# Gather of four items at once from a two-part split of the unnormalised rows, extra items beside their expert, filler products on TensorE in the routing

## The reference

```python
for l in range(DEPTH):                                   # DEPTH = 1
    h = x + hybrid_mixer(rmsnorm(x, norm_mix_g[l]), ...)
    x = h + hierarchical_moe(rmsnorm(h, norm_ffn_g[l]), ...)
return rmsnorm(x, final_norm_g)

def hierarchical_moe(xn, rg_w, rg_b, re_w, re_b, w1, w3, w2):
    ...
    e_w = e_top / jnp.sum(e_top, axis=-1, keepdims=True) * g_top
    expert_id = g_idx * EXPERTS_PER_GROUP + e_idx        # 1 of 4 groups, 2 of its 8 experts
    gate = jnp.sum(jax.nn.one_hot(expert_id, N_EXPERTS, dtype=f32) * e_w[..., None], axis=1)
    h = jax.nn.silu(jnp.einsum('td,edf->tef', t, w1)) * jnp.einsum('td,edf->tef', t, w3)
    h = h * gate[:, :, None].astype(h.dtype)
    y = jnp.einsum('tef,efd->td', h, w2)
```

## Time and profile before

| what | value |
|---|---|
| median of 3 runs | 1475.35 us (1474.34 to 1475.4) |
| profiled execution, its own time | 1474.14 us |
| span from first to last instruction | 1472.3 us |
| mean granted TensorE clock | 0.985 |
| PE busy, share of the span | 94% |
| DVE, ACT, POOL busy | 37%, 25%, 15% |
| chain that ended last | PE 58%, DMA 21% |
| read from HBM | 481.53 MB |

### The profile page before, as it was taken

How to read it: one execution, slowest core, us unless ns; L and a number is a source line. 1 busy time by engine, 2 the same in 40 slices (tenths; PEclk the granted TensorE clock), 3 DMA queues, 4 the chain that set the end, 5 groups by cost and what they waited for, 6 DMA issues and landing times.

```text
span 1472.3 us, 20876 instructions
## 1 busy us (share of the span) xinstructions
PE 1379.7 (94%) x8358; PEld 786.9 (53%) x8358; DVE 540.8 (37%) x1072; ACT 366.5 (25%) x625; POOL 214.4 (15%) x198
## 2 busy tenths in 40 slices
PE   6999899998896899999999999999999999999996
PEld 5874697896685444443543444435434444354343
DVE  4899710415413523322323223223232232232325
ACT  3010168565555211111102111111021111110212
POOL 2000356576684100000000000000000000000000
PEclk9999999999998899999999999999999999999998
DMA  8433444334357599999999999999999999999993
GB/s 208 170 115 114 144 175 144 126 131 168 115 214 300 243 422 427 427 426 423 428 426 427 425 428 426 426 424 427 427 427 423 427 426 426 426 427 428 427 423 136
DMA packets 80682, 484.19 MB, mean 329 GB/s; under 512 B 17393, under 2 KB 17474, under 8 KB 46210
## 3 DMA queue, kind: packets, MB, share of 16 engines
q1 hardware_dynamic: 79842, 481.28, 80.1%
q10 hardware_dynamic: 672, 2.10, 0.4%
q0 software_dynamic: 128, 0.26, 0.1%
HBM read 481.53 MB, written 2.10 MB: 328 GB/s over the span
## 4 chain that ended last, share of the span: by engine, by line
PE 58%; DMA 21%; DVE 3%; ACT 2%; issue 1%; POOL 0%; DVEq 0%; ACTq 0%
PE ps L1750 22%; DMA ring<-in_expert_w_dram 21%; PE ps L1413 11%; PE ps L1768 9%; PE ps L1728 6%; PE ps L1758 3%; PE ps L1779 2%; PE ps L1780 1%; PE ps L1740 1%; ACT reg_t L786 1%; DVE reg_e L1074 0%; PE ps L1678 0%; DVE reg_y L1036 0%; ACT reg_d L785 0%; DVE reg_x L1356 0%
## 5 line engine op out<-in xcount | busy, mean ns | idle before, releaser
L1750 PE MATMUL ps<-ring,reg_y 128*64 128x512 f32 x1056 | 240.1, 598 | 31.6 <-DMA ring<-in_expert_w_dram 31.6
L1750 PE MATMUL ps<-reg_e,reg_y 128*64 128x512 f32 x1056 | 234.6, 593 | 0.8 <-DVE reg_y L1274 0.8
L1768 PE MATMUL ps<-ring,reg_y 128*64 128x512 f32 x1056 | 233.5, 595 | 0.8 <-DVE reg_y L1289 0.8
L528 POOL TENSOR_TENSOR w_lo<-ring,w_hi 128x512 fp32r<-128x512 f32 x144 | 183.6, 1303 | 90.8 <-ACT w_hi L585 89.1
L1295 DVE TENSOR_TENSOR y_lo_t<-ps,y_hi_t 64x512 fp32r<-64x512 f32 x132 | 90.9, 689 | 213.0 <-ACT y_hi_t L815 211.7
L1750 PEld LDWEIGHTS ps<-ring,reg_y 128*64 128x64 f32 x1056 | 70.6, 136 | 183.3 <-issue 128.8
L815 ACT ACTIVATE y_hi_t<-ps 64x512 fp32r<-64x512 f32 x132 | 78.1, 591 | 335.0 <-PE ps L1768 332.6
L1750 PEld LDWEIGHTS ps<-reg_e,reg_y 128*64 128x64 f32 x1056 | 74.6, 137 | 154.7 <-issue 143.4
L1768 PEld LDWEIGHTS ps<-ring,reg_y 128*64 128x64 f32 x1056 | 72.9, 137 | 134.7 <-issue 132.0
L1304 DVE TENSOR_TENSOR reg_x<-ps,reg_x 128x512 f32<-128x512 f32 x136 | 87.3, 684 | 121.6 <-PE ps L1780 121.6
L1285 DVE TENSOR_SCALAR reg_y<-ps,lamv 128x512 f32<-128x512 f32 x33 | 24.8, 751 | 256.4 <-PE ps L1750 256.4
(11 more groups left out here) (355 smaller groups left out, 1507.8 us busy)
## 6 DMA issues: line engine op xcount, KB each, us to landing
ring<-in_expert_w_dram SPq DMA_DIRECT2D x132, 2048.0 KB, 22.5
reg_e<-in_expert_w_dram SPq DMA_DIRECT2D x66, 2048.0 KB, 23.6
ring<-in_w_in_dram SPq DMA_DIRECT2D x20, 2048.0 KB, 8.0
ring<-in_w_out_dram SPq DMA_DIRECT2D x8, 2048.0 KB, 8.0
reg_x<-in_x_dram SPq DMA_DIRECT2D x4, 1024.0 KB, 8.4
out_dram<-reg_x SPq DMA_DIRECT2D x4, 512.0 KB, 2.7
reg_e<-in_ssm_w_glu_dram ACTq DMA_DIRECT2D x1, 1024.0 KB, 5.9
reg_d<-in_final_norm_g_dram ACTq DMA_DIRECT2D x1, 1024.0 KB, 4.7
```

The source lines that it names most:

```text
L528: G.tensor_tensor(w_lo[:, i % BUFS, :], unit(u % SLOTS_A)[:, c, :], w_hi[:, i % BUFS, :], ALU.subtract).then_inc(row_lo, 1)
L1750: last = M(psb[m][64 * i:64 * i + 64, :], xeT[:, cc, 64 * q:64 * q + 64], unit(s)[:, c, :], start=cc < 2, stop=cc >= DC - 2)
L1768: last = M(psb[3 + i // 2][64 * (i % 2):64 * (i % 2) + 64, :], hT[:, 2 * half + f, :], unit2(s)[:, f, 512 * i:512 * i + 512], start=half = ...
```

## The change

- Rows are split into two parts in the type that PE multiplies in one pass (`h_hi`, `h_lo`), straight from h without the factor 1/rms. ACT (`h_high`) and DVE (`h_low`) do it column group by column group as the last projections end. POOL has no part in it. The factor 1/rms is gathered with the gates and applied where ACT and DVE copy the results of w1 and w3 (`a_up`, `v_up`).
- `gather` serves four items (`QG`): 16 blocks x 2 parts x 2 halves = 64 products of 256 columns, once in two passes. `gates` sums two numbers a slot for four items. DVE makes `selS` from two numbers a token (`x_r`).
- Items stand in expert order: an extra item comes right after its expert's first item. SP loads an expert once (`item(first item's number, e)`); the slot of unit k is given back by the expert's last item. POOL watches the transfers and tells PE by `e_in`, which counts items, not experts. With 33 items, item 17 is the extra one of expert 16, and the one that is left for a pass of its own is item 32, expert 31.
- The router's chain loses the gates' placing and gains the items' numbering before the slots are chosen; numbers of extra items come later.
- `keep_clock` issues 6 and 3 products whose result nobody reads, before and behind the ranking.
- The rows of w2 are dealt to partitions in another order, so that each partition reads one run of memory a unit; ACT and DVE read the results of w1 and w3 with a step of four values for it.
- The last norm's weights are loaded by SP at the end, into a free weight slot.

```diff
+QG = 4
+HG = QG // QE
 ITERS = NE // QE
+GROUPS = NE // QG
 PASSES = T // SLOT
 EXTRA = 8
+ITEMS = NE + EXTRA
...
-        w2_v = e_w2.rearrange("l e (h c p) n -> p (l e) h c n", h=2, p=P)
+        w2_v = e_w2.rearrange("l e (p h c) n -> p (l e) h c n", h=2, p=P)
...
-            with sp.Fori(0, NE) as e:
-                item(e, e)
-            sp.wait_ge(rk_ready, 2)
...
+            item(0, 0)
+            sp.wait_ge(rk_ready, 1)
+            with sp.Fori(1, NE) as e:
+                item(sp.value_load(c_int[0:1, ds(e, 1)], min_val=1, max_val=ITEMS - 1), e)
+            sp.wait_ge(slot_free, (sp.value_load(n_extra[0:1, 0:1], min_val=0, max_val=EXTRA - 1) + NE) * 6 + 1)
+            sp.dma_start(fg, final_g.unsqueeze(0).broadcast_to([P, D])).then_inc(fg_in, 16)
...
+            def item_landed(e):
+
+                for k in range(6):
+                    s = slot_of(k)
+                    base = 16 * (UNITS_A // SLOTS_A) if s < SLOTS_A else 0
+                    g.wait_ge(ring_in[s], e * 16 + base + 16)
+                    g.sem_inc(e_in, 1)
+
+            item_landed(0)
+            g.wait_ge(rk_ready, 2)
+            with g.Fori(1, ITEMS) as i_:
+                item_landed(g.value_load(ids[0:1, ds(i_, 1)], min_val=0, max_val=NE - 1))
...
+            def h_high(k):
+                for b in range(TB):
+                    A.activation(h_hi[:, b, :, 32 * k:32 * k + 32], h_columns(b, k), cp).then_inc(hp_hi, 1)
...
-                A.activation(a1, psb[0][:, :], cp).then_inc(e_a1, 1)
+                a.wait_ge(e_gsev, g_ + 1)
+                A.activation(v3(a1, P), psb[0][:, :].rearrange("p (q f) -> p f q", f=EC), cp,
+                             scale=g_slot[:, q, 0:1]).then_inc(e_a1, 1)
...
+            def h_low(k):
+
+                v.wait_ge(hp_hi, TB * (k + 1))
+                for b in range(TB):
+                    V.tensor_tensor(h_lo[:, b, :, 32 * k:32 * k + 32], h_columns(b, k), h_hi[:, b, :, 32 * k:32 * k + 32],
+                                    ALU.subtract).then_inc(hp_lo, 1)
...
+            link(V.tensor_scalar(x_n, cnt, float(SLOT), 1.0, ALU.is_gt, ALU.add))
+            for k in range(2, PASSES):
+                link(V.scalar_tensor_tensor(x_n, cnt, float(SLOT * k), x_n, ALU.is_gt, ALU.add))
+            link(V.tensor_tensor_scan(x_e, ones[:, 0:NE], x_n, 0.0, ALU.mult, ALU.add))
+            link(V.scalar_tensor_tensor(x_p, x_c.unsqueeze(1).broadcast_to([P, TB, NE]), float(SLOT), rk, ALU.mult, ALU.add))
+            link(V.scalar_tensor_tensor(x_p, x_p, 1.0, sel, ALU.add, ALU.mult))
+            V.reduce_max(x_r[:, :, 0:1], x_p, axis=AX)
+            link(V.reduce_sum(x_sum, x_p, axis=AX))
+            link(V.tensor_tensor(x_r[:, :, 1:2], x_sum, x_r[:, :, 0:1], ALU.subtract))
...
+                w = nq * SLOT
+                out = [selS[:, b, 0:nq, :].rearrange("p q s -> p (q s)") for b in range(TB)]
                 for b in range(TB):
+                    last = V.tensor_scalar(out[b], iota_q[:, 0:w], x_r[:, b, 0:1], None, ALU.is_equal)
+                step(last, g_, 2)
...
+            def v_gather(g_, nq):
+                w = nq * SLOT
+                for m in range(DC // 2):
+                    v.wait_ge(e_gath, g_ * 8 + m + 1)
+                    V.tensor_tensor(xeT[m // 4][:, 2 * (m % 4):2 * (m % 4) + 2, 0:w],
+                                    v3(psb[(0, 1, 5)[m % 3]][:, :], QG * SLOT)[:, :, 0:w],
+                                    g_rows[:, 2 * m:2 * m + 2].unsqueeze(2).broadcast_to([P, 2, w]), ALU.mult).then_inc(e_gev, 1)
...
+            def keep_clock(n_):
+
+                for _i in range(n_):
+                    M(psb[7][:, :], ident[:, :], xt[:, 0, 0:512], start=True, stop=True)
+
+            keep_clock(6)
...
+            def gather(g_, nq):
+                w = nq * SLOT
+                pe.wait_ge(e_sel, g_ + 1)
...
-                    for part in (hi, mid, lo):
+                    for part in (h_hi, h_lo):
                         for b in range(TB):
-                            last = M(psb[bank][:, (c % 4) * P:(c % 4) * P + ns], part[:, b, c * P:(c + 1) * P],
-                                     selS[:, b, 0:ns // SLOT, :].rearrange("p q s -> p (q s)"), start=k == 0, stop=k == 5)
+                            last = M(bank[:, o:o + w], part[:, b, c, :], selS[:, b, 0:nq, :].rearrange("p q s -> p (q s)"),
+                                     start=k == 0, stop=k == 3)
...
+            keep_clock(3)
+            pe.wait_ge(hp_lo, 4 * TB)
+            pe.wait_ge(id_r, 1)
+            gather(0, QG)
+            pe_items(0, 0, 0, 0, QE, first=True)
+            for h in range(1, HG):
+                pe_items(h, 0, QE * h, h, QE)
+            with pe.Fori(1, GROUPS) as it:
+                for h in range(HG):
+                    pe_items(it * HG + h, it, it * QG + QE * h, h, QE)
```

More of the change, by code:

```diff
@@ L1749, in up @@
                         i = c % 2
-                        last = M(psb[m][64 * i:64 * i + 64, :], xeT[:, cc, 64 * q:64 * q + 64], unit(s)[:, c, :],
+                        last = M(psb[m][64 * i:64 * i + 64, :], xeT[half][:, c, 64 * q:64 * q + 64], unit(s)[:, c, :],
                                  start=cc < 2, stop=cc >= DC - 2)
@@ L1821, in pe_items @@
                     down(n0 + 1)
[L1823 to L1827 removed]
+            keep_clock(3)
[3 more added lines that the diff above has]
+            pe_items(0, 0, 0, 0, QE, first=True)
+            for h in range(1, HG):
+                pe_items(h, 0, QE * h, h, QE)
+            with pe.Fori(1, GROUPS) as it:
+                for h in range(HG):
+                    pe_items(it * HG + h, it, it * QG + QE * h, h, QE)
+            pe.wait_ge(rk_ready, 1)
             extra = pe.value_load(n_extra[0:1, 0:1], min_val=0, max_val=EXTRA - 1)
```

375 lines of the change are left out of this document (167 added, 208 removed).

## The result

| | before | after |
|---|---|---|
| median of 4 runs each, side by side | 1474.84 us | 1465.42 us (1462.96 to 1466.02) |
| ratio | | 0.9933, 95% interval 0.9919 to 0.9947 |
| profiled execution, its span | 1474.14, 1472.3 | 1466.02, 1463.5 |

What follows compares the result with a forecast made beforehand. Transfers bound the experts' part, PE being 5% under them. Terms -5.9 - 29.5 + 15.4 + 2.7 + 4.1 + 0.5 = -12.7 us from 1474.14 gave 1461.4, the median 1.2 above; forecast 1462 us, range 1454 to 1469.

Steps and rivals of the forecast that it cites:

- The start, -5.9: Routing up to the first item: `up` of item 0 begins at 485.9 instead of 491.78, -5.9 us, needing the full clock.
- rival 1: Routing gives less: clock lost and a numbering chain 2 us longer; start -1, total about -8, 1467 us; 12 in 100.
- The gather, 64 products in 7.7: Gather for four items: 64 one-pass products of 256 columns at 0.12 us each, 7.7 us.
- Rival 4: Gathers: each new product costs 0.24 us, a gather 15.4; together +25, slower at 1487 us; 5 in 100.
- The load, -29.5: Middle of the experts' part: expert 16 is loaded once, 32 loads instead of 33, -29.5 us.
- the stop, +15.4: Behind expert 16, transfers stand still until item 17 frees a slot: +15.4 us; zero is the preceding item's last unit landing.
- Rival 3: Passes after item 17: PE does not catch up, transfers wait again in the next gathers; +1.4, 1477 us; 6 in 100.
- w2's runs, costed at nothing: Experts' transfers: w2's longer runs change nothing, since the full rate already has the shorter runs in it; 0 us.
- The last passes, +2.7: Behind PE's last wait: gather of 7.7 for 5.45 and 0.5 for twice the gates, +2.7 us.
- the small parts, +0.5: Behind the last wait: POOL's hop between transfer and PE, and copies reading PSUM four values apart, +0.5 us (0 to 1.5).
- The last gather, +4.1: Last item's own gather: 64 products of 64 columns, then gates and copies; last combine at 1460.2 instead of 1456.14, +4.1 us.
- DVE's hidden part: Pass without a gather: 1.2 us for the hidden part that the gather had covered, with PE still faster than the transfers.

Runs made afterwards that it cites:

- e7: The changed kernel with twelve one-pass products of 512 columns added in each pass that has a gather, to make PE later: 1474.62 us, ratio 1.0001.
- e1: The changed kernel with the old order of w2's rows and straight copies of the w1 and w3 results: 1469.09 us, ratio 0.9962.
- e4: The changed kernel loading expert 16 once for each of its two items, with SP waiting for the item list: 1496.89 us, ratio 1.0147.
- e5: The changed kernel with one filler ahead of the last logits, seven instead of six behind them, four instead of three behind the ranking: 1463.98 us, ratio 0.9928.
- e4b: The changed kernel with expert 16 loaded again for item 17, load order written out as constants so nothing waits: 1476.69 us, ratio 1.0016.
- e2: The kernel before with only the new order of w2's rows and the stepped PSUM copies it needs: 1469.32 us, ratio 0.9955.
- e9: The changed kernel with six one-pass filler products of 512 columns where PE waited for DVE in the last item's own gather: 1461.88 us, ratio 0.9923.
- e6: The changed kernel without the gather, gates and slot choice for a nonexistent item behind the last item: 1455.03 us, ratio 0.9876.

## Why the prediction was right, and where it was not

**The bound.** Right. Transfers set the middle: the number of units, the stop, the rate and PE's two ends account for the 8.8 us of span to within about 1 us, and e7's delays of PE cost nothing in the passes ahead of the stop.

**The start, -5.9, mis-sized.** Measured -3.85, of which 1.1 is where the stretch happened to begin; by the table it is 30.19 - 27.47 = -2.7 for these two executions, -4.4 where the clock held to the end of the logits in both kernels (30.19 - 25.8) and -3.2 where it fell in them in both (30.63 - 27.47). The prediction put the fillers behind the last logits and looked for idle gaps behind them ("The idle gaps left are 0.3 and 0.8"). The gap that mattered was ahead of them, the 1.07 us in which PE waits for the turned columns. The earlier trace rows have it as 0.97, and there the clock fell at 468.1, 2.7 us behind the start of the last logits. The prediction put this down to the idle time behind the logits; but e1, e4 and e7 have fillers in that place and the clock fell 2.0 to 2.7 us behind that start all the same. At the lower clock the fillers ended 2.1 us after DVE's choice. This is the lost clock of rival 1, at about half its size. e5 takes it away, 2.0 us. Of the 1.2 that are left of the miss, about 0.3 is DVE's scaling of the logits (3.4 behind their start, where 1.0 later than the 2.1 of before had been forecast) and 0.7 lies between the ranking and the gather, 4.56 us instead of 3.9. The POOL-free steps took 0.2 as forecast.

**The gather, 64 products in 7.7.** Right: 0.12 us each at 256 columns, and 0.112 at 64 columns, where the bf16 products of before took 0.030 (six in 0.18 from 1450.53 on). The weight loads are busy all the time beside them (4.00 of 4.00 us in the window from 1438), which fits the prediction's reading that the weights set the price; no run takes it apart. Rival 4 is out. Its own sum was about 3 too small: by its terms the end would have been +7.7 in the last full gather and +4.9 (from +4.1 to the +9 named) in the last item's, not +9.4 in all.

**The load, -29.5, and the stop, +15.4.** Right in mechanism. The load put back costs 12.2 by the medians and 13.2 by the profiles (e4b), and e1, which has the rate of before, is 12.8 under the kernel before from the next issue to the last wait (909.11 - 896.30); 14.1 had been forecast for the two terms together. So the stop with its knock-on is 16 to 17, and the slice gives 17.7: the term was 1 to 2 too small. PE's side was within 0.1 (it enters item 16's pass 11.4 behind zero and gives back the first slot after 42.5; forecast 11.3 and 42.5). What is off lies in the transfers. Zero is 937.7 (two units behind the wait at 927.86), and zero plus 29.5 is 967, but by the windows the bytes ended at about 964.1 (344 of 429 GB/s from 960 to 965). They flowed again from about 981.8 (275 of 429 from 980 to 985), where the forecast means 982.6 (a landing at 49.8, and the 4.9 of one unit before it). Why they ended 3 us earlier than forecast is not taken apart. e7 shows that the stop follows PE's lateness one for one. Rival 3 is out: no second slice of the change is low, and only e7, with PE made later, shows the beginning of such a dip.

**w2's runs, costed at nothing: the step that was wrong.** "w2's longer runs (the full rate of the earlier trace rows has the shorter runs in it)" excluded a slower rate, but not a faster one. e1 and e2 show -3.8 and -4.6. This one gain covers the stop's and half of the end's misses; without it the change is at 1469 (e1), the edge of the range. That the total came within 3.4 us of the forecast is luck to this extent: a gain that had not been forecast stood against a start that gained less and a stop and an end that cost more.

**The last passes, +2.7, and the small parts, +0.5.** Measured 2.8 for both; the stepped copies cost nothing, so the +0.5, an allowance taken from what a step in SBUF costs, was not needed. POOL as a hop between transfer and PE has 1.24 to 1.26 us of idle time at the waits, as the earlier trace rows have.

**The last gather, +4.1, mis-sized.** Measured +7.0 and another +1.8 in the combine behind it. The step "from 1454.5 five column pairs of 0.96" took the full clock for granted. The pairs came 1.70 apart from the fourth on, where the clock fell. Of the 4.7 us that are missing with the combine's, e9 gives 3.1 back. e6 showed that the term need not be there at all.

**DVE's hidden part.** The wait for it in the second item of a pass without a gather, named in the prediction as 1.2, is 1.01 at 993.39, and hidden under the transfers as forecast.

## What to carry to other kernels

When a transfer is dropped from a stream whose issues wait for buffers to come free, the gain is less than the transfer's own time (here 12 to 13 of 29.5 us): ask when the next issue is released, and take the difference of the landings. Look at the wait ahead of the place where the clock falls as well as at the idle time behind it: here the fillers behind the logits did not keep the clock up, they only brought it back before the gather, and the one in the wait ahead of the logits kept it. A filler's length must be worked out at the lower clock too, or it turns into the wait. An edit that lengthens the runs of a transfer that is the bound has to be priced in both directions, since half a per cent of a 900 us stream is as large as the other terms.

## What the runs showed of the hardware that was not expected

- Transfers of w2 with one run of memory for each partition and unit move 428 to 429 GB/s where the former order moved 426 (windows of 420 and 410 us), both in the changed kernel (71374 packets against e1's 79566) and in the kernel before (e2's 72234 against 80682).
- Behind the same wait of 1.06 to 1.08 us ahead of the last logits the granted clock fell in all eight executions of the changed code without a filler ahead, in five within the logits and in three 2.0 to 2.7 us behind their start, each time with PE busy from the wait to the fall. Behind before's 0.97 it fell at 468.1, and in e2 within the logits. With 0.20 in its place it held in both executions.
- It also fell at the end of the last gather of e9, 64 one-pass products of 64 columns and six of 512 from 1433.05 on (at about 1441.6), with no idle time among them.
- Reading PSUM with a step of four values cost DVE (0.751) and ACT (0.597) nothing on 128 x 512; a copy of ACT with a factor of its own for each partition took 0.687 with and without the step (the change, e1).
